# Two transformer parts on one core: the order around the unnormalised blocks, and fp32 matmuls of 256 columns issued as two of 128

## The chip, the cores and the metric

The kernel runs on one core of one Trainium2 chip. The metric is the device time of one execution in microseconds (us). All work is fp32 in the reference; the kernel holds everything in one program for one core.

## The reference

The input is one sequence of 256 tokens of width 1024. A first part of two layers is followed by two hybrid layers.

```python
for layer in range(2):
    shift_m, scale_m, gate_m, shift_f, scale_f, gate_f = ada_mod(c, ada_w[layer], ada_b[layer])
    h = modulate(rms_norm(x, norm_gains[layer, 0]), shift_m, scale_m)
    y = attn_hybrid_mixer(...) if layer == 0 else retention_mixer(...)
    x = x + gate_m * y
    h = modulate(rms_norm(x, norm_gains[layer, 1]), shift_f, scale_f)
    x = x + gate_f * swiglu(h, ffn_w_gate_up[layer], ffn_w_down[layer])
...
return rms_norm(x, final_norm)
```

`rms_norm` divides each token by the root of the mean of its squares and multiplies with a gain; `modulate(h, shift, scale)` is `h * (1 + scale) + shift`; `swiglu` is `(silu(h @ gate) * (h @ up)) @ down`, 2816 wide. `retention_mixer` projects h to q, k, v and g, turns q and k by position, and runs retention over four heads. Each hybrid layer joins a convolution branch, a latent attention branch (eight heads, `mla`) and a dilated attention branch (24 heads, `dil`) behind one normalised input and one wide projection.

## The kernel before, in words

x is kept transposed, as 8 tiles of 128 features by 256 tokens. A weight block is 128 x 1024 numbers, that is eight 128 x 128 tiles. There are 444 blocks, which pass through four slots. SyncE loads a block into `raw`; ScalarE rounds it to the high part `whi` (`hi(n)`, L1149); VectorE takes the rest as the low part `wlo` (`lo(n)`, L1647). TensorE multiplies with three matmuls per weight tile, high by high, high by low and low by high (`run`, L512 to L514). The activations have high and low parts too (`h[:, k, 0:T]` and `h[:, k, T:2T]`, T = 256). These are the dense runs: 24 matmuls of 256 columns for a block with one output tile. The waits on `blk_done`, `w_lo`, `slot_free`, `un_hi`, `h_ready` and so on, written out by hand on each engine, and the order of the instructions in each engine's queue set the order of all work.

An output tile lies in one of two banks of PSUM (`G`, by the parity of its number g). TensorE may write a bank again once `slot_free` tells that the tile two before has been read. `S` has three banks, used by attention scores and, in bank 2, by the sum of squares of x (a matmul with a matrix of ones), from which ScalarE makes the reciprocal root of the mean (`root`, L1157 and L1159).

At two places the first four blocks of a projection start before the root is known: at the retention projection (B_RET) behind the first down projection, and at the second gate/up projection (B_FFN1) behind the retention's output projection. `run_unnormed` multiplies them with x times gain, unnormalised (258 columns: 256 tokens, and the shift as two more). Its first pass covers blocks e = 0 and 1 together over k = 0 to 7 (L615), then comes the sum of squares (L618, L620), the low matmuls of both (L625), and then blocks 2 and 3 (L633 to L635). The ends are taken out of PSUM by `raw_out` (L1318 and L1319) on ScalarE and multiplied with the root later by `by_root` (L1903) on VectorE. Meanwhile `entry_norm` on VectorE makes the normalised tiles, `sq` (L1892) and from these the low parts of `h` (L1897), while `norm_hi` on ScalarE makes the high parts (L1168); block 4 is the first that uses them. At B_FFN1 the first two gate/up pairs go through `by_root`, a silu and `up_gate` (L1981) before the loop over the others starts.

`x_update` on VectorE adds each finished tile of a down or output projection to x (L1850), makes the low part of the unnormalised tile (`un_low`, L1831) and adds its squares up (L1838); `x_squares` on ScalarE makes the high part (L1301) and the squares (L1152). Between them VectorE works off dot products for the modulation vectors (`ada_later`, L1655), at blocks given by tables such as DOWN0_DOTS.

Small fp32 matmuls, not split into parts, stand between the dense runs of 24: `ret_sum` and `ret_scores` in retention; `d_sums` (a sum of squares over a head, 256 columns, L1017), `mla_scores` (128 and 256 columns, L1048 and L1049), `mla_transposes` (four of 128 columns, L1009) and others in the hybrid layers.

Of the kernel before, what the change touches and what calls it, by code (L numbers as in the profile page):

```python
# [125 lines left out]
DOWN0_DOTS = {2 * n: [57 + n] for n in range(11)}  # L126
# [67 lines left out]
def build(nc, a, out):  # L194
# [8 lines left out]
    with ctx:  # L203
# [289 lines left out]
        def _(pe):  # L493
# [109 lines left out]
            def run_unnormed(b, g, n, src):  # L603


                o = [G[:, (g + e) % 2, 0:U_WIDE] for e in range(2)]
                for e in range(2):
                    pe.wait_ge(slot_free[(g + e - 2) % 4], taken(g + e - 2))
                pe.wait_ge(w_lo, b + 2)
                pe.wait_ge(shift_lo, n + 1)  # L610
                for k in range(KT):
                    pe.wait_ge(un_hi, 8 * n + k + 1)
# [4 lines left out]
                pe.wait_ge(sq_summed, n + 2)  # L617
                pe.matmul(S[:, 2, 0:T], ones[:, :], sq[:, 0, :], start=True, stop=False)  # L618
                pe.wait_ge(sq_ready, 8 * (n + 2) + KT)
                pe.matmul(S[:, 2, 0:T], ones[:, :], sq[:, KT - 1, :], start=False, stop=True).then_inc(ss_done, 1)  # L620
# [7 lines left out]
                for e in (2, 3):  # L628
                    pe.wait_ge(slot_free[(g + e - 2) % 4], taken(g + e - 2))
                    pe.wait_ge(w_lo, b + e + 1)  # L630
                    for k in range(KT):
                        wh, wl = (w[:, (b + e) % 4, k * P:(k + 1) * P] for w in (whi, wlo))
                        pe.matmul(o[e - 2], wh, src[:, k, 0:U_WIDE], start=(k == 0), stop=False)  # L633
                        pe.matmul(o[e - 2], wh, src[:, k, U_LOW:U_LOW + U_WIDE], start=False, stop=False)
                        ins = pe.matmul(o[e - 2], wl, src[:, k, 0:U_WIDE], start=False, stop=(k == KT - 1))  # L635
# [257 lines left out]

            def ret_sum(hh):

                slot = use_t()
                pe.wait_ge(r_added, hh + 1)
                pe.matmul(Tp[:, slot, 0:T], ones[:, :], sq[:, 4, :], start=True, stop=True).then_inc(t_done, 1)
# [26 lines left out]
            for l in range(LAYERS2):  # L925
# [28 lines left out]
                def entry_sums():  # L954
# [3 lines left out]
                    pe.matmul(S[:, 2, 0:T], ones[:, :], sq[:, 0, :], start=True, stop=False)  # L958
                    ins = pe.matmul(S[:, 2, 0:T], ones[:, :], sq[:, KT - 1, :], start=False, stop=True)
                    if l == 0:  # L960
                        pe.wait_ge(sqf_summed, 1)
                        pe.wait_ge(sqf_ready, 8)
                        pe.matmul(S[:, 1, 0:T], ones[:, :], sqf[:, 0, :], start=True, stop=False)
                        ins = pe.matmul(S[:, 1, 0:T], ones[:, :], sqf[:, KT - 1, :], start=False, stop=True)
# [1546 lines left out]
```

## Time and profile before

| | |
|---|---|
| median of 3 runs | 1472.85 us (1468.15 to 1475.81) |
| profiled execution, its own time | 1468.51 us |
| its span, first to last instruction | 1466.7 us |
| TensorE busy | 1438.4 us, 98% |
| VectorE busy | 1043.1 us, 71% |
| ScalarE busy | 849.5 us, 58% |
| GpSimd busy | 93.6 us, 6% |
| mean granted TensorE clock | 0.998 of full |

The profile is of one execution. Busy time of TensorE counts overlapping matmuls once, and a matmul's duration is longer than the distance from its start to the next one's, since matmuls are pipelined. So in what follows time on TensorE is read from start to start, or as idle time ahead of an instruction.

### The profile page before, as it was taken

Reading aid. Unit: us, or ns where it says so; the run is one execution under the profiler, and the core shown is the slowest. Engines: PE = TensorE matmul, PEld = TensorE weight load, DVE = VectorE, ACT = ScalarE, POOL = GpSimd, SP = SyncE. Lnnn points to the kernel's source line nnn. Section 1 sums busy time; section 2 is a strip of 40 time slices with the busy share of each in tenths; the row PEclk is TensorE's granted clock in tenths of the full one; section 3 lists DMA queues with packets and bytes.
Section 4 is the critical chain, followed back from the end, with each engine's and each line's share of the span. In section 5 each row is a group of like instructions: output and inputs, shape, how many; then the busy total and the mean of one; then the engine's idle time right before and its main releaser. Section 6 shows DMA issues by size and latency. Waiting matters only on the chain.

```text
span 1466.7 us, 30157 instructions
## 1 busy us (share of the span) xinstructions
PE 1438.4 (98%) x11556; PEld 1361.7 (93%) x11556; DVE 1043.1 (71%) x1861; ACT 849.5 (58%) x1482; POOL 93.6 (6%) x136
## 2 busy tenths in 40 slices
PE   8999999998999999999999999999999999999999
PEld 6887999998979998999998989899999898989999
DVE  2888898887786677755665857886676684787664
ACT  4565666555556656445565766565566576656553
POOL 0111011110000000000020000230000000031000
PEclk9999999999999999999999999999999999999999
DMA  9866699996675465666663555336666355433663
GB/s 364 324 211 220 225 331 339 343 329 202 217 229 154 134 202 182 210 195 193 195 234 113 172 160 158 93 111 196 194 193 214 106 170 170 144 102 121 193 194 126
DMA packets 81185, 292.04 MB, mean 199 GB/s; under 512 B 9185, under 2 KB 10465, under 8 KB 80946
## 3 DMA queue, kind: packets, MB, share of 16 engines
q1 hardware_dynamic: 68274, 244.31, 51.4%
q0 software_dynamic: 11792, 42.77, 8.8%
q10 hardware_dynamic: 1008, 3.41, 0.7%
q8 instruction: 79, 1.29, 0.4%
q14 instruction: 32, 0.26, 0.1%
HBM read 289.40 MB, written 1.05 MB: 198 GB/s over the span
## 4 chain that ended last, share of the span: by engine, by line
PE 85%; DVE 9%; ACT 3%; issue 2%; DMA 0%; SPq 0%; DVEq 0%; ACTq 0%
PE G L512 21%; PE G L513 21%; PE G L514 21%; DVE wlo L1647 3%; PE G L571 3%; PE G L573 3%; PE G L572 3%; PE Tp L1017 1%; ACT whi L1149 1%; PE O L1093 1%; PE G L593 1%; PE Tp L945 1%; PE S L995 1%; DVE aw L1655 1%; PE Tp L685 1%
## 5 line engine op out<-in xcount | busy, mean ns | idle before, releaser
L1647 DVE TENSOR_TENSOR wlo<-raw,whi 128x1024 fp32r<-128x1024 f32 x444 | 545.4, 1231 | 261.0 <-ACT whi L1149 259.3
L512 PE MATMUL G<-h,whi 128*128 128x256 f32 x2064 | 587.2, 284 | 8.6 <-DVE wlo L1647 2.3
L1149 ACT ACTIVATE whi<-raw 128x1024 fp32r<-128x1024 f32 x444 | 468.9, 1058 | 216.6 <-PE G L514 161.6
L513 PE MATMUL G<-h,whi 128*128 128x256 f32 x2064 | 571.7, 277 | 0.0
L514 PE MATMUL G<-h,wlo 128*128 128x256 f32 x2064 | 571.6, 277 | 0.0
L512 PEld LDWEIGHTS G<-h,whi 128*128 128x128 f32 x2064 | 388.0, 188 | 16.4 <-issue 5.0
L513 PEld LDWEIGHTS G<-h,whi 128*128 128x128 f32 x2064 | 388.1, 188 | 1.8 <-issue 0.5
L514 PEld LDWEIGHTS G<-h,wlo 128*128 128x128 f32 x2064 | 387.7, 188 | 0.0
L1655 DVE CUSTOM_DVE_ANT_0 aw<-aw,cs,cols 128x1024 f32<-128x1024 f32 x80 | 101.4, 1279 | 0.0
L512 PE MATMUL G<-ah,whi 128*128 128x256 f32 x352 | 97.2, 276 | 0.0
L513 PE MATMUL G<-ah,whi 128*128 128x256 f32 x352 | 97.2, 276 | 0.0
L514 PE MATMUL G<-ah,wlo 128*128 128x256 f32 x352 | 97.2, 276 | 0.0
L488 POOL TENSOR_TENSOR bias<-dist,slopes 128x256 f32<-128x256 f32 (+1 forms) x48 | 48.7, 1030 | 533.2 <-DVE mn L2248 524.8
L512 PE MATMUL G<-yh,whi 128*128 128x256 f32 x288 | 79.9, 277 | 0.0
L513 PE MATMUL G<-yh,whi 128*128 128x256 f32 x288 | 79.5, 276 | 0.0
L514 PE MATMUL G<-yh,wlo 128*128 128x256 f32 x288 | 79.5, 276 | 0.0
L571 PE MATMUL G<-whi,h 128*128 128x512 f32 x192 | 76.9, 401 | 0.9 <-ACT rv L1182 0.5
L471 POOL DMA_DIRECT2D aw<-in_ada x80 | 42.5, 532 | 544.8 <-DVE mod L1655 510.8
L573 PE MATMUL G<-wlo,h 128*128 128x512 f32 x192 | 75.7, 394 | 0.0
L572 PE MATMUL G<-whi,h 128*128 128x512 f32 x192 | 75.5, 393 | 0.0
L513 PEld LDWEIGHTS G<-ah,whi 128*128 128x128 f32 x352 | 66.1, 188 | 0.0
L512 PEld LDWEIGHTS G<-ah,whi 128*128 128x128 f32 x352 | 66.1, 188 | 0.0
(393 smaller groups left out, 2314.4 us busy)
## 6 DMA issues: line engine op xcount, KB each, us to landing
raw<-in_w SPq DMA_DIRECT2D x444, 512.0 KB, 4.1
aw<-in_ada POOLq DMA_DIRECT2D x80, 512.0 KB, 5.2
adaw<-in_ada SPq DMA_DIRECT2D x8, 1024.0 KB, 15.3
sn<-in_uq ACTq DMA_DIRECT2D x2, 768.0 KB, 4.6
x<-in_x SPq DMA_DIRECT2D x1, 1024.0 KB, 5.2
pt<-in_ukv ACTq DMA_DIRECT2D x2, 512.0 KB, 5.8
out<-x SPq DMA_DIRECT2D x4, 256.0 KB, 2.3
dec<-in_dec ACTq DMA_DIRECT2D x1, 512.0 KB, 7.2
```

Of the source, the lines that this page charges most:

```text
L471: pool.dma_start(aw[:, r % ADA_SLOTS, :], a["ada"][16 + r]).then_inc(ada_raw[r % ADA_SLOTS], 16)
L488: pool.tensor_tensor(bias[:, DIST[grp]], dist[:, DIST[grp]], slopes[:, c:c + 1].broadcast_to([P, w]), ALU.mult).then_inc(bias_ready, 1)
L512: pe.matmul(o, wh, mv[:, 0:T], start=(k == 0), stop=False)
L513: pe.matmul(o, wh, mv[:, T:2 * T], start=False, stop=False)
L514: ins = pe.matmul(o, wl, mv[:, 0:T], start=False, stop=(k == k_of - 1))
L571: pe.matmul(o, hh, wh, start=(k == 0), stop=False)
L572: pe.matmul(o, hl, wh, start=False, stop=False)
L573: ins = pe.matmul(o, hh, wl, start=False, stop=(k == KT - 1))
L593: pe.matmul(o[n], w[:, slot, k * P:(k + 1) * P], src[:, k, 0:T], start=(k == 0 and w is whi), stop=False)
L1149: act.activation(whi[:, s, :], raw[:, s, :], ACT.Copy).then_inc(w_hi, 1)
L1647: dve.tensor_tensor(wlo[:, s, :], raw[:, s, :], whi[:, s, :], ALU.subtract).then_inc(w_lo, 1)
L1655: return dve.tensor_tensor_reduce(out=w, in0=w, in1=cs[:, :], scale=1.0, scalar=cols[:, C_ADAB + n:C_ADAB + n + 1], op0=ALU.mult, op1=ALU.add,
```

## The change

It has these parts.

1. `run_unnormed`: block 1's output goes to bank 0 of S in place of the other bank of G, and TensorE waits ahead of the first pass for one bank only. The sum of squares moves ahead of k = 7 of the first pass.
2. ScalarE: the root moves ahead of the first `raw_out`; copies out, high parts and weight splits are dealt anew. The first looped gate/up group of B_FFN1 is written out, with the second `ah` activation put into it.
3. VectorE: `x_update` adds a tile's squares behind its `un_low`, no longer ahead of the next x tile; the eleven dots of the down projection stand at blocks 0, 1, 2, 4, ... 18 in place of 0, 2, ... 20. `entry_norm` splits block b + 5 between h tiles 3 and 4; the splits of blocks 6 and 7 and the products with the root are dealt anew.
4. `in_halves`: fp32 matmuls of 256 columns in `d_sums`, `mla_scores`, `ret_sum` and `entry_sums` are issued as two of 128.

```diff
-DOWN0_DOTS = {2 * n: [57 + n] for n in range(11)}
+DOWN0_DOTS = {b: [57 + n] for n, b in enumerate((0, 1, 2, 4, 6, 8, 10, 12, 14, 16, 18))}
...
-                o = [G[:, (g + e) % 2, 0:U_WIDE] for e in range(2)]
-                for e in range(2):
-                    pe.wait_ge(slot_free[(g + e - 2) % 4], taken(g + e - 2))
+                o = [G[:, g % 2, 0:U_WIDE], S[:, 0, 0:U_WIDE]]
+                pe.wait_ge(slot_free[(g - 2) % 4], taken(g - 2))
                 pe.wait_ge(w_lo, b + 2)
                 pe.wait_ge(shift_lo, n + 1)
                 for k in range(KT):
+                    if k == KT - 1:
+                        pe.wait_ge(sq_summed, n + 2)
+                        pe.matmul(S[:, 2, 0:T], ones[:, :], sq[:, 0, :], start=True, stop=False)
+                        pe.wait_ge(sq_ready, 8 * (n + 2) + KT)
+                        pe.matmul(S[:, 2, 0:T], ones[:, :], sq[:, KT - 1, :], start=False, stop=True).then_inc(ss_done, 1)
                     pe.wait_ge(un_hi, 8 * n + k + 1)
...
+            def in_halves(to, w, moving, start):
+
+                for o in (0, P):
+                    ins = pe.matmul(to[:, o:o + P], w, moving[:, o:o + P], start=start, stop=True)
+                return ins
...
-                    pe.matmul(Tp[:, slot, 0:T], bones[:, :], sq[:, j % 8, :], start=True, stop=True).then_inc(t_done, 1)
+                    in_halves(Tp[:, slot, 0:T], bones[:, :], sq[:, j % 8, :], True).then_inc(t_done, 1)
...
             hi(B_RET + 3)
+            root(2)
             raw_out(B_RET, G_RET, 0, rqk[:, 0, :])
+            hi(B_RET + 4)
             raw_out(B_RET, G_RET, 1, rqk[:, 1, :])
-            root(2)
-            hi(B_RET + 4)
             norm_hi(16, 16, 48, range(4))
             hi(B_RET + 5)
+            raw_out(B_RET, G_RET, 2, rqk[:, 2, :])
             norm_hi(16, 16, 48, range(4, KT))
...
-                            if m >= 2:
+                            if m >= 2 and not unnormed:
                                 add_squares(m - 1)
...
                         un_low(ends.index(bb))
+                        if 1 <= ends.index(bb) < KT - 1:
+                            add_squares(ends.index(bb))
...
                 for k in range(KT):
+                    if k == 4:
+                        lo(b + 5)
                     dve.wait_ge(hi_ready, 8 * n - 8 + k + 1)
...
-            by_root(rqk[:, 0, :], G_RET).then_inc(q_scaled, 1)
-            by_root(rqk[:, 1, :], G_RET + 1).then_inc(q_scaled, 1)
-            lo(B_RET + 5)
-            for b in (2, 3):
+            for b in range(4):
+                if b < 2:
+                    lo(B_RET + b + 6)
                 by_root(rqk[:, b, :], G_RET + b).then_inc(q_scaled, 1)
-                lo(B_RET + b + 4)
```

ScalarE's queue at B_RET, before, from the last weight rounding ahead of the copies out (`whi`, L1149), over the copies (`hb` and `rqk`), to the root (`rstd`) and the high parts of h:

```order
L1149 ACTIVATE whi<-raw 128x1024
L1318 ACTIVATE hb<-G 128x1
L1319 ACTIVATE rqk<-G 128x256
L1318 ACTIVATE hb<-G 128x1
L1319 ACTIVATE rqk<-G 128x256
L1157 ACTIVATE rstd<-S 128x256
L1159 ACTIVATE rstd<-rstd 128x256
L1149 ACTIVATE whi<-raw 128x1024
L1168 ACTIVATE h<-sq,mod 128x256 x4
L1149 ACTIVATE whi<-raw 128x1024
L1168 ACTIVATE h<-sq,mod 128x256 x4
```

The same place after the change, where the lines have other numbers (L1158 is `hi`, L1166 and L1168 the root, L1328 and L1329 `raw_out`, L1177 `norm_hi`):

```order
L1158 ACTIVATE whi<-raw 128x1024
L1166 ACTIVATE rstd<-S 128x256
L1168 ACTIVATE rstd<-rstd 128x256
L1328 ACTIVATE hb<-G 128x1
L1329 ACTIVATE rqk<-G 128x256
L1158 ACTIVATE whi<-raw 128x1024
L1328 ACTIVATE hb<-S 128x1
L1329 ACTIVATE rqk<-S 128x256
L1177 ACTIVATE h<-sq,mod 128x256 x4
L1158 ACTIVATE whi<-raw 128x1024
L1328 ACTIVATE hb<-G 128x1
L1329 ACTIVATE rqk<-G 128x256
```

The root stands ahead of all copies, the second copy reads S, and the third copy stands ahead of the last four h tiles.

VectorE's queue at B_RET, before, from the last dot (`aw`) and the last update of x to the first products with the root (`rqk`):

```order
L1655 ISA aw,mod<-aw,cs,cols 128x1024
L1655 ISA mod 128x1
L1838 TENSOR_TENSOR sq<-sq 128x256
L1850 SCALAR_TENSOR_TENSOR x<-G,mod,x 128x256
L1831 SCALAR_TENSOR_TENSOR yr<-x,modA,yr 128x256
L1647 TENSOR_TENSOR wlo<-raw,whi 128x1024
L1892 SCALAR_TENSOR_TENSOR sq<-x,modA,rstd 128x256 x8
L1647 TENSOR_TENSOR wlo<-raw,whi 128x1024
L1897 SCALAR_TENSOR_TENSOR h<-sq,mod,h 128x256 x8
L1903 TENSOR_TENSOR rqk<-rqk,rstd 128x256 x2
```

The same place after (L1670 is `lo`, L1873 the update of x, L1854 `un_low`, L1917 and L1924 `entry_norm`, L1930 `by_root`):

```order
L1670 TENSOR_TENSOR wlo<-raw,whi 128x1024
L1873 SCALAR_TENSOR_TENSOR x<-G,mod,x 128x256
L1854 SCALAR_TENSOR_TENSOR yr<-x,modA,yr 128x256
L1670 TENSOR_TENSOR wlo<-raw,whi 128x1024
L1917 SCALAR_TENSOR_TENSOR sq<-x,modA,rstd 128x256 x8
L1670 TENSOR_TENSOR wlo<-raw,whi 128x1024
L1924 SCALAR_TENSOR_TENSOR h<-sq,mod,h 128x256 x4
L1670 TENSOR_TENSOR wlo<-raw,whi 128x1024
L1924 SCALAR_TENSOR_TENSOR h<-sq,mod,h 128x256 x4
L1670 TENSOR_TENSOR wlo<-raw,whi 128x1024
L1930 TENSOR_TENSOR rqk<-rqk,rstd 128x256
```

The dot and the sum of squares no longer stand ahead of the last update of x, and a split stands in the middle of the h tiles.

## Rows read from the trace of the kernel before

**Rows 1.** The page: span, the chain that ended last, one dense group.

```profile
span 1466.7 us, 30157 instructions
...
PE 85%; DVE 9%; ACT 3%; issue 2%; DMA 0%; SPq 0%; DVEq 0%; ACTq 0%
...
L513 PE MATMUL G<-h,whi 128*128 128x256 f32 x2064 | 571.7, 277 | 0.0
```

**Rows 2.** Timeline of TensorE at B_RET: start us, us, [idle before <-releaser].

```profile
346.52 0.28 PE L514 MATMUL G<-ah,wlo 128*128 128x256 f32 x1
348.53 0.36 PE L615 MATMUL G<-yr,whi 128*128 128x258 f32 x1 [1.74 <-issue]
...
362.12 0.39 PE L512 MATMUL G<-h,whi 128*128 128x256 f32 x1 [0.88 <-ACT rqk L1319]
...
366.20 0.36 PE L512 MATMUL G<-h,whi 128*128 128x256 f32 x1 [1.08 <-DVE wlo L1647]
```

**Rows 3.** Timeline of TensorE at B_FFN1.

```profile
548.87 0.28 PE L514 MATMUL G<-yr,wlo 128*128 128x256 f32 x1
549.77 0.36 PE L615 MATMUL G<-ah,whi 128*128 128x258 f32 x1 [0.62 <-issue]
...
563.35 0.38 PE L512 MATMUL G<-h,whi 128*128 128x256 f32 x1 [0.92 <-ACT sg L1319]
...
567.42 0.36 PE L512 MATMUL G<-h,whi 128*128 128x256 f32 x1 [0.98 <-DVE wlo L1647]
...
571.91 0.38 PE L512 MATMUL G<-h,whi 128*128 128x256 f32 x1 [1.52 <-ACT sg L1326]
```

**Rows 4.** The chain that ended last, at B_RET: start us, us, what.

```profile
348.53 4.11 PE G L615 x32
...
353.51 1.95 PE G L625 x16
...
356.23 0.43 ACT rstd L1159
356.68 3.26 DVE sq L1892 x8
359.94 1.14 DVE wlo L1647
361.08 3.17 DVE h L1897 x8
```

**Rows 5.** Timeline of VectorE ahead of B_RET.

```profile
346.41 1.28 DVE L1655 CUSTOM_DVE_ANT_0 aw<-aw,cs,cols 128x1024 f32<-128x1024 f32 x1
...
347.95 0.47 DVE L1850 SCALAR_TENSOR_TENSOR x<-G,mod,x 128x256 f32<-128x256 f32 x1
```

**Rows 6.** Timeline of ScalarE, at B_RET and at B_FFN1.

```profile
357.51 1.69 ACT L1168 ACTIVATE h<-sq,mod 128x256 fp32r<-128x256 f32 x4
...
565.53 1.28 ACT L1408 ACT_TABLE_LOAD   x1
```

**Rows 7.** Windows of TensorE: busy us (matmuls), granted clock, DMA share, GB/s.

```profile
521.00:548.00 27.00, 27.00 (x232) 1.00 0.68 218
600.00:627.00 27.00, 27.00 (x241) 1.00 0.63 194
```

**Rows 8.** Timeline of TensorE around three `d_sums` of the second hybrid layer.

```profile
1188.33 0.60 PE L1017 MATMUL Tp<-sq,bones 128*128 128x256 f32 x2
...
1191.49 0.59 PE L1017 MATMUL Tp<-sq,bones 128*128 128x256 f32 x2
1191.74 0.47 PE L512 MATMUL G<-h,whi 128*128 128x256 f32 x1
...
1194.75 0.38 PE L1017 MATMUL Tp<-sq,bones 128*128 128x256 f32 x1
```

**Rows 9.** Timeline of TensorE around one `mla_transposes`, four matmuls of 128 columns.

```profile
837.71 0.60 PE L1009 MATMUL Tp<-ident,qk 128*96 128x128 f32 x4
838.07 0.37 PE L512 MATMUL G<-h,whi 128*128 128x256 f32 x1
```

More of the change, by code:

```diff
@@ L897, in ret_sum @@
                 pe.wait_ge(r_added, hh + 1)
-                pe.matmul(Tp[:, slot, 0:T], ones[:, :], sq[:, 4, :], start=True, stop=True).then_inc(t_done, 1)
+                in_halves(Tp[:, slot, 0:T], ones[:, :], sq[:, 4, :], True).then_inc(t_done, 1)
             for b in range(48):
@@ L957, in entry_sums @@
                     pe.wait_ge(sq_ready, 8 * (5 + l))
-                    pe.matmul(S[:, 2, 0:T], ones[:, :], sq[:, 0, :], start=True, stop=False)
-                    ins = pe.matmul(S[:, 2, 0:T], ones[:, :], sq[:, KT - 1, :], start=False, stop=True)
+                    for o in (0, P):
+                        pe.matmul(S[:, 2, o:o + P], ones[:, :], sq[:, 0, o:o + P], start=True, stop=False)
+                        ins = pe.matmul(S[:, 2, o:o + P], ones[:, :], sq[:, KT - 1, o:o + P], start=False, stop=True)
                     if l == 0:
@@ L962, in entry_sums @@
                         pe.wait_ge(sqf_ready, 8)
-                        pe.matmul(S[:, 1, 0:T], ones[:, :], sqf[:, 0, :], start=True, stop=False)
-                        ins = pe.matmul(S[:, 1, 0:T], ones[:, :], sqf[:, KT - 1, :], start=False, stop=True)
+                        for o in (0, P):
+                            pe.matmul(S[:, 1, o:o + P], ones[:, :], sqf[:, 0, o:o + P], start=True, stop=False)
+                            ins = pe.matmul(S[:, 1, o:o + P], ones[:, :], sqf[:, KT - 1, o:o + P], start=False, stop=True)
                     ins.then_inc(ss_done, 1)
@@ L1395, in _ @@
             hi(B_FFN1 + 3)
+            root(3)
             raw_out(B_FFN1, G_FFN1, 0, sg[:, 0, :])
+            hi(B_FFN1 + 4)
             raw_out(B_FFN1, G_FFN1, 1, af[:, 0, :])
-            root(3)
-            hi(B_FFN1 + 4)
             norm_hi(24, 24, 72, range(4))
             hi(B_FFN1 + 5)
+            raw_out(B_FFN1, G_FFN1, 2, sg[:, 1, :])
             norm_hi(24, 24, 72, range(4, KT))
-            for b in (2, 3):
-                raw_out(B_FFN1, G_FFN1, b, (sg if b == 2 else af)[:, 1, :])
-                hi(B_FFN1 + b + 4)
+            raw_out(B_FFN1, G_FFN1, 3, af[:, 1, :])
+            hi(B_FFN1 + 6)
             for q in range(2):
@@ L1408, in _, with early_high @@
                 act.activation(sg[:, q, :], sg[:, q, :], ACT.Silu, bias=scol[:, 2 * q:2 * q + 1]).then_inc(gate_silu, 1)
-            for q in range(2):
+            hi(B_FFN1 + 7)
+            def early_high(q):
                 act.wait_ge(up_done, q + 1)
                 act.activation(ah[:, q, 0:T], af[:, q, :], ACT.Copy).then_inc(ah_hi, 1)
-            ffn(B_FFN1, G_FFN1, 1)
+            early_high(0)
+            gate_up(B_FFN1, G_FFN1, 1, between=lambda: early_high(1))
+            ffn(B_FFN1, G_FFN1, 2)
             def entry_tile(l, m, g, r4):
```

51 lines of the change are left out of this document (26 added, 25 removed).

## The prediction, made before the changed kernel had run

> **What bounds the kernel now.** I read the page first. TensorE is busy in nearly the whole span and the chain of work that ended last lies on it for 85% of the time [rows 1]. So the kernel is bound by TensorE, and only two things can shorten it: less time for the same matmuls, or fewer stretches in which TensorE waits. The granted clock is 1.00, the 2.4 GHz level, in every stretch I looked at [rows 7], so the clock is no lever.
>
> Then I read TensorE's timeline around the two places where `run_unnormed` stands, since the change rewrites them. At the first (B_RET) the last matmul of the down projection starts at 346.52 and the first of the unnormalised blocks at 348.53. Later block 4 starts at 362.12 after 0.88 us idle, and block 5 at 366.20 after 1.08 us idle [rows 2]. The first break is 2.01 us from start to start with 1.74 us idle; inside a dense run that distance is at most 0.12 us, so a break costs 2.01 - 0.12 - 1.74 = 0.15 us beyond its idle time. The three then cost 3.70 + 0.45 = 4.2 us. At the second place (B_FFN1) there are four, with 0.62, 0.92, 0.98 and 1.52 us idle [rows 3]: 4.04 + 0.60 = 4.6 us. Together 8.8 us, the most that the new order can bring.
>
> What ends those waits is in the chain [rows 4]. The 32 matmuls of the first pass take 4.11 us, the sum of squares stands behind them (0.87 us, from 352.64 to 353.51), then 16 low matmuls take 1.95 us. Only then, behind two copies out, comes the root on ScalarE (ends 356.66), and from there VectorE alone carries the chain: eight scaled tiles 3.26 us, a weight split 1.14 us, eight h tiles 3.17 us. The first wait has another cause. VectorE runs a dot of 1.28 us from 346.41 and updates the last x tile only from 347.95 to 348.42 [rows 5]; TensorE starts 0.11 us after that, since its second output goes to the bank which that update reads.
>
> **The change, part by part.**
>
> *The second output moves to a bank of S.* TensorE no longer waits for the last x tile at the start. It starts at about 346.7 at the first place, which saves 1.8 us, and some 0.75 us at the second. The tile is needed at k = 7, after 28 of 32 matmuls, 28/32 x 4.11 = 3.6 us later (350.3). With the last dot taken away, VectorE can update x at 346.9 (0.47 us), and ScalarE needs two activations of 0.42 us (1.69 / 4, [rows 6]): ready at about 348.3, so nothing waits. The dots moved to the first blocks cost VectorE 1.28 us each in stretches of three blocks (8.2 us) where it has room. Without it TensorE would lose at most their length, 2.6 us.
>
> *The sum of squares moves ahead of k = 7, and the root ahead of the copies.* The sum ends at 351.2 instead of 353.5, its result is there some 0.2 us later, and VectorE begins its tiles at about 352.2 instead of 356.68. That is 4.5 us earlier, of which 1.8 is TensorE's earlier start.
>
> Now TensorE's own time against VectorE's. TensorE: k = 7 and the 16 low matmuls to 353.6, then 48 matmuls of blocks 2 and 3 at 0.121 us each (1.95 / 16) to 359.4. VectorE: 352.2 + 3.26 = 355.4, split for block 4 to 356.6, h 0 to 3 to 358.2, split for block 5 to 359.3, h 4 to 7 to 360.9. TensorE reaches h tile 4 at 359.4 + 12 x 0.113 = 360.8 and the tile was ready at about 359.8: no wait. Block 5 starts at 362.1 with its weights long there. Both later waits go.
>
> What is late next is the bank for block 6 (wanted at 364.9). It is freed by ScalarE's copy of block 4, which stands behind the four bias additions, and these wait for VectorE's four products with the root: VectorE has a split (1.14), a product (0.33), a split (1.14) and three products (1.0) behind h 7, so 364.8, then one bias and one copy (0.8): 365.6. **A new wait of about 0.75 us; the first place brings 4.2 - 0.75 = 3.4 us.**
>
> At the second place the same arithmetic starts 0.75 us earlier: last matmul at 548.87, squares at 552.6, VectorE's tiles from 554.6, blocks 2 and 3 done at 561.7, blocks 4 and 5 without a wait to 567.1. The table load of 1.28 us on ScalarE [rows 6] now ends at about 564.6, and the silu behind it holds VectorE for 0.8 us. Its chain of 15.5 us of work (3.2 + 1.1 + 3.2 + 1.1, products, gates, four more splits, lows) plus 0.8 brings the bank of the first looped up block free at 571.1. TensorE wants it at 569.9. Of 4.6 us I leave 1.2: **3.4 us.**
>
> *Two of 128 for one of 256.* The code's fp32 matmul shows as two instructions in the profile. 74 are halved: 48 in `d_sums`, 16 in `mla_scores`, 4 in `ret_sum`, 6 in `entry_sums`. The direct cost: the pair of 256 starts 0.25 us ahead of the next matmul, which then takes 0.47 us, 0.72 in all [rows 8]. Four of 128 start 0.36 us ahead of one that takes 0.37 us, 0.73 in all [rows 9]. So 0.01 us each, 0.7 us for 74.
>
> The possible return is a pace. Dense runs go at one of two: in 27 us TensorE ran 232 matmuls in one stretch and 241 in others, all at full clock [rows 7], 3.8% apart (0.118 and 0.113 us start to start). Behind `d_sums` the pace alternates: from one to the next it is 3.16 us, then 3.26 us [rows 8], so a slow block of 24 costs 0.10 us. So it goes on through both layers: 14 of the 28 stretches directly behind a `d_sums` are slow, the last of them behind 1191.49. Behind four 128-column matmuls the next matmul is short and the stretch fast [rows 9], always in both layers (8 of 8), though each had a `d_sums` ahead of them. Halving it could turn all 14 (1.4 us) and, if `mla_scores` behaves the same, some 8 stretches' worth more (0.8 us). Bounds: -2.2 + 0.7 = -1.5 us if all turn fast; +0.7 us if the alternation stays; +2.1 us if every stretch turns slow (14 more). I take -0.6, nearer to rows 9, which are the same stream but for being transposes.
>
> The Trainium skill (TensorE: Matmul & The Clock Gate, "Back-to-back issue gap") gives a gap of N/2.4 + 2.5 ns, so every extra matmul instruction costs 2.5 ns and the same columns never get cheaper by being cut: an estimate by it is 74 x 2 x 2.5 ns = 0.4 us lost and none returned, a total of -6.4 us. [...]
>
> **Sum.** -3.4 - 3.4 - 0.6 = -7.4 us. The profiled execution took 1468.5 us (span 1466.7 and 1.8 around it), so it would take 1461.1. That execution stands at the low end of the runs shown, 4.3 us under their median of 1472.85; moved along, the median becomes **1465 us**.
>
> **Rivals.** *The supply takes the place of the waits* (chance 0.19). ScalarE and VectorE get no lighter, and at both places they run nearly without pause for 12 us. If raw copies and splits queue a little worse than I count, only the starts are gained, 1.8 + 0.75, with 1 us of the rest: -3.5 us, 1469.
>
> *A long stretch changes pace* (0.19). From 571.91, after a wait of 1.52 us [rows 3], to the end of the down projection some 163 us later, TensorE ran at the fast pace (600 to 627 in rows 7 is of it). With that wait changed it may settle at the slow one: 163 x 3.8% = +6.2 us, so -1.2 us in all, 1471.5. For it: half of the stretches behind `d_sums` are slow, and the stretch from 521 to 548 [rows 7] stayed slow for long. Against: after most waits the fast one set in.
>
> *Everything comes* (0.13): no new waits, all stretches fast: -8.8 - 1.5 = -10.3 us, 1462.5.
>
> *Slower* (0.05): the slow pace takes the long stretches of the last layers too. There are 3 x 2064 = 6192 matmuls on h [rows 1]; if 4000 of them, those behind the first changed place by my estimate, ran at 0.118 in place of 0.113 us (3.8%, 0.0043 us each), that is +17.2 us, so 1482.5. The time is above before's once 7.4 / 0.0043 = 1700 have turned, and by over 0.5% from 3400.
>
> *Forecast* (0.44): 1465, its own range 1461.5 to 1468.5.
>
> **Range and chances.** The tails take the slow-stretch case in and leave out the slower one: 1459 to 1472. 0.5% is 7.4 us, about what a measurement of this kernel can tell from no change, and the forecast lies on it. Faster by more: 0.7 of the forecast and the whole of the everything case, 0.44. Slower by more: 0.05. Within: 0.51.
>
> **What would show it.** In the changed profile: the first unnormalised matmul within 0.3 us of the last one of the down projection; the root ending by 352.2; no break ahead of blocks 4 and 5; a short one ahead of block 6 and one of about 1 us in the first looped gate/up group; `d_sums` as four instructions, and the distance between them 3.17 us at every one that only a block of 24 parts. Wrong would make it: matmuls of 0.28 us that run at 0.118 start to start after 571, breaks at k = 7, or `d_sums` distances that alternate still.

## The result, and the profile after

The changed kernel took 1464.58 us in the median of 12 runs (1461.10 to 1468.31), before 1474.92 us beside it; the ratio is 0.9935, 95% interval 0.9917 to 0.9953. Timed twice more, unchanged, it gave 0.9963 (0.9942 to 0.9985) and 1.0006 (0.9984 to 1.0027). The mean of the three ratios is 0.9968, 4.7 us. The ratios stand as they were recorded with their intervals and are not quotients of the two medians. So the first result stands at the favourable end of what the change is worth, and a good part of this text is about why three such measurements differ.

The page of the profiled execution, which took 1464.42 us, to be read against [rows 1]:

```profile
span 1462.6 us, 30445 instructions
...
PE 89%; DVE 7%; ACT 2%; issue 2%; DMA 0%; SPq 0%; DVEq 0%; ACTq 0%
...
L513 PE MATMUL G<-h,whi 128*128 128x256 f32 x2064 | 572.8, 278 | 0.0
```

TensorE now carries 89% of the chain, VectorE 7% instead of 9%. But the same 2064 matmuls last 278 ns in the mean instead of 277: something was given back inside the dense runs.

TensorE's timeline at B_RET and B_FFN1 after the change (columns as in [rows 2]):

```profile
346.68 0.28 PE L514 MATMUL G<-ah,wlo 128*128 128x256 f32 x1
346.79 0.28 PE L619 MATMUL G<-yr,whi 128*128 128x258 f32 x1
...
365.58 0.38 PE L512 MATMUL G<-h,whi 128*128 128x256 f32 x1 [0.69 <-ACT rqk L1401]
...
544.05 0.28 PE L619 MATMUL G<-ah,whi 128*128 128x258 f32 x1
...
565.97 0.39 PE L512 MATMUL G<-h,whi 128*128 128x256 f32 x1 [1.06 <-DVE af L1901]
```

Of seven breaks two are left. The first unnormalised matmul starts 0.11 us behind the last one of the down projection, where it was 2.01 us [rows 2]. Blocks 4 and 5 have none, at either place; block 6 has one at B_RET, block 7 one at B_FFN1.

The chain at B_RET, then ScalarE's and VectorE's timelines there, to be read against [rows 4] and [rows 5]:

```profile
350.33 0.43 PE S L613 x2
350.76 0.43 PE S L615 x2
```

```profile
351.23 0.38 ACT L1166 ACTIVATE rstd<-S 128x256 f32<-128x256 f32 x1 [1.96 <-PE S L615]
351.65 0.42 ACT L1168 ACTIVATE rstd<-rstd 128x256 f32<-128x256 f32 x1
...
363.95 1.31 ACT L1372 ACTIVATE rqk<-rqk,hb 128x256 f32<-128x256 f32 x3 [0.96 <-DVE rqk L1930]
365.17 0.36 ACT L1401 ACTIVATE rqk<-G 128x256 f32<-128x256 f32 x1
```

```profile
346.99 0.48 DVE L1873 SCALAR_TENSOR_TENSOR x<-G,mod,x 128x256 f32<-128x256 f32 x1 [0.34 <-PE G L514]
...
352.10 3.26 DVE L1917 SCALAR_TENSOR_TENSOR sq<-x,modA,rstd 128x256 f32<-128x256 f32 x8 [1.56 <-ACT rstd L1168]
...
363.50 1.09 DVE L1930 TENSOR_TENSOR rqk<-rqk,rstd 128x256 f32<-128x256 f32 x3
```

The last x tile is updated from 346.99 to 347.47 us while TensorE is already in the first pass. The sum of squares ends at 351.19, VectorE starts its eight tiles at 352.10 where it was 356.68. The last lines of both engines are the new wait: products to 364.59, bias additions to 365.26, the copy that frees the bank to 365.53, and TensorE 0.05 us after it.

### The profile page after: what moved, and what is told of

Same layout as the page of the kernel before. It is cut to its first block, busy times and chain, and to the rows that moved or that the text cites. A ratio compares the mean times of both kernels' runs of the same rounds, so it can differ in the third digit from the quotient of the medians.

```text
span 1462.6 us, 30445 instructions
## 1 busy us (share of the span) xinstructions
PE 1441.0 (99%) x11704; PEld 1371.9 (94%) x11704; DVE 1043.7 (71%) x1861; ACT 848.6 (58%) x1482; POOL 92.0 (6%) x136
## 4 chain that ended last, share of the span: by engine, by line
PE 89%; DVE 7%; ACT 2%; issue 2%; DMA 0%; SPq 0%; DVEq 0%; ACTq 0%
PE G L512 22%; PE G L513 22%; PE G L514 22%; PE G L571 3%; PE G L572 3%; PE G L573 3%; DVE wlo L1670 2%; PE Tp L898 2%; PE O L1102 1%; PE G L593 1%; ACT whi L1158 1%; PE Tp L952 1%; PE S L1004 1%; DVE aw L1678 1%; PE Tp L686 1%
## 5 line engine op out<-in xcount | busy, mean ns | idle before, releaser
L1670 DVE TENSOR_TENSOR wlo<-raw,whi 128x1024 fp32r<-128x1024 f32 x444 | 546.0, 1232 | 257.2 <-ACT whi L1158 255.4
L1158 ACT ACTIVATE whi<-raw 128x1024 fp32r<-128x1024 f32 x444 | 468.8, 1058 | 216.7 <-PE G L514 160.7
L512 PE MATMUL G<-h,whi 128*128 128x256 f32 x2064 | 583.5, 283 | 4.8 <-DVE at L2319 1.6
L514 PE MATMUL G<-h,wlo 128*128 128x256 f32 x2064 | 572.8, 278 | 0.0
L512 PEld LDWEIGHTS G<-h,whi 128*128 128x128 f32 x2064 | 389.4, 189 | 10.6 <-issue 2.2
L514 PEld LDWEIGHTS G<-h,wlo 128*128 128x128 f32 x2064 | 387.8, 188 | 0.0
L512 PE MATMUL G<-ah,whi 128*128 128x256 f32 x352 | 97.2, 276 | 0.0
L514 PE MATMUL G<-ah,wlo 128*128 128x256 f32 x352 | 97.2, 276 | 0.0
L512 PE MATMUL G<-yh,whi 128*128 128x256 f32 x288 | 80.2, 278 | 0.0
L514 PE MATMUL G<-yh,wlo 128*128 128x256 f32 x288 | 80.0, 278 | 0.0
L571 PE MATMUL G<-whi,h 128*128 128x512 f32 x192 | 76.8, 400 | 1.4 <-ACT mqk L1267 1.4
L573 PE MATMUL G<-wlo,h 128*128 128x512 f32 x192 | 75.6, 394 | 0.0
L512 PEld LDWEIGHTS G<-ah,whi 128*128 128x128 f32 x352 | 66.1, 188 | 0.0
```

The lines of the kernel that those rows point to most:

```text
L512: pe.matmul(o, wh, mv[:, 0:T], start=(k == 0), stop=False)
L514: ins = pe.matmul(o, wl, mv[:, 0:T], start=False, stop=(k == k_of - 1))
L571: pe.matmul(o, hh, wh, start=(k == 0), stop=False)
L573: ins = pe.matmul(o, hh, wl, start=False, stop=(k == KT - 1))
L1158: act.activation(whi[:, s, :], raw[:, s, :], ACT.Copy).then_inc(w_hi, 1)
L1670: dve.tensor_tensor(wlo[:, s, :], raw[:, s, :], whi[:, s, :], ALU.subtract).then_inc(w_lo, 1)
```

## The experiments

**How they are compared.** The spread of the runs of one program (7 to 18 us in these measurements) is larger than most effects here. The traces show what makes up most of it from one profiled execution to another; the other executions have no trace. In a dense run the next matmul starts either 112 to 115 ns or 116 to 119 ns after the one before, and a long run stays with one distance for hundreds of matmuls. In this text these two distances are the two paces, and a start of the second kind is a slow start. Windows of 27 us in after, one in the loop behind B_FFN1 and one in the merge of the first hybrid layer (about 975 to 1080 us), then the second window in the kernel before:

```profile
600.00:627.00 27.00, 27.00 (x241) 1.00 0.60 193
990.00:1017.00 27.00, 27.00 (x232) 1.00 0.59 188
```

```profile
990.00:1017.00 27.00, 27.00 (x241) 1.00 0.65 198
```

The clock is granted in full (1.00) in all of them. So beside the times I give for each profile the span less 4.4 ns (118 less 113.6) for each slow start, counted over the whole trace, called here the span at one pace. (A count over all matmuls, whatever their shape, is 106 to 132 starts higher, in all profiles nearly alike.) It still holds waits that differ from one execution to another of kernels that are alike there: up to 1.1 us ahead of 340 us and up to 1.6 us between the two changed places, among them one of the retention (ahead of L571, at about 418 us). So it is good to some 1 to 2 us only. The last three columns leave these waits out: the matmuls of the dense runs (L512 to L514) are matched one to one with those of the kernel before, slow starts counted out, and each column is what a profile gained on before in one stretch, from 340 to 380 us (B_RET), from 548 to 580 us (B_FFN1) and from 580 us to the end, by before's times.

| profile | span | slow starts | span at one pace | B_RET | B_FFN1 | behind 580 |
|---|---|---|---|---|---|---|
| before | 1466.7 | 1548 | 1459.9 | | | |
| f4_before_again | 1467.0 | 1802 | 1459.1 | 0.0 | 0.1 | 0.0 |
| f1_order_only | 1460.2 | 1836 | 1452.1 | 3.5 | 3.7 | 0.0 |
| f2_halves_only | 1475.4 | 3365 | 1460.6 | 0.1 | 0.1 | -0.9 |
| after | 1462.6 | 2317 | 1452.4 | 3.5 | 3.8 | -1.0 |
| f3_after_again | 1466.1 | 2974 | 1453.0 | 3.5 | 3.8 | -1.1 |
| h5_after_third | 1463.2 | 2002 | 1454.4 | 3.5 | 3.7 | -0.9 |
| g1_bank_only | 1465.9 | 2121 | 1456.6 | 2.0 | 1.0 | 0.1 |
| g2_sum_and_root_first | 1470.4 | 3267 | 1456.0 | 2.2 | 2.4 | 0.1 |
| g3_order_plus | 1458.9 | 1752 | 1451.2 | 4.4 | 4.6 | -0.4 |
| h2_order_tuned | 1459.5 | 1649 | 1452.2 | 4.5 | 4.4 | -0.5 |
| h3_tuned_steered | 1470.2 | 3935 | 1452.9 | 4.0 | 4.0 | -1.4 |
| h4_before_steered | 1485.9 | 5528 | 1461.6 | -0.3 | -0.5 | -1.0 |

My theory: the order is worth what its breaks were, and the halves cost a little and return nothing. Rivals: the gain comes from the pace, by the halves or by chance; the bank alone or the earlier root alone makes it.

### The order alone, the halves alone, and both kernels again

f1_order_only is after with `in_halves` taken out:

```diff
-                    in_halves(Tp[:, slot, 0:T], bones[:, :], sq[:, j % 8, :], True).then_inc(t_done, 1)
+                    pe.matmul(Tp[:, slot, 0:T], bones[:, :], sq[:, j % 8, :], start=True, stop=True).then_inc(t_done, 1)
```

and so in `mla_scores`, `ret_sum` and `entry_sums`. f2_halves_only is the kernel before with the same lines the other way round. f3_after_again and f4_before_again are after and before unchanged.

> The new order (parts 1 to 3) with the fp32 matmuls left whole at 256 columns. Theory: nearly all of the gain is the removed breaks. The changed kernel's profile had matmuls of the same ordinal 3.3 us earlier behind the first place and 3.7 us earlier over the second one. So this kernel's profile shows about 7 us won at the two places, breaks of about 0.9 us at block 6 (first place) and 1.2 us at block 7 (second place) left, and a time 6 to 9 us under before. Rival (the halved matmuls carry a good part of the 9.5 us): only 3 to 5 us under before.

> The kernel before, with only the fp32 matmuls of 256 columns halved (d_sums, mla_scores, ret_sum, entry_sums). Theory: nothing, within 1.5 us of before, since the stretches behind a lone d_sums turn fast (14 slow ones, 1.4 us) while the eight behind d_sums and four transposes turn slow (0.8 us) and the halving costs 0.01 us each (0.7 us). Rival (the halves set the pace of the long stretches too): 3 us or more under before, with no slow stretch of over 100 matmuls in the hybrid layers.

> The changed kernel once more, unaltered. Theory (the pace of a long stretch is drawn anew in each execution): the stretch of 888 matmuls in the first hybrid layer's merge, slow in the first profile (3.7 us), is fast in this one or other long stretches are slow, and the ratio to before is 0.993 to 0.996. Rival (the pace is fixed by the program): the same stretches slow as in the first profile, to the matmul.

> The kernel before once more, unaltered. Theory (pace drawn anew): long stretches change pace against the first profile, whose span of 1466.7 us was at the low end of its runs (1468 to 1483 us); a typical execution has one or two more long stretches slow and a span of about 1472. Rival (fixed by the program): the same slow stretches, and the longer runs come from elsewhere, such as longer breaks.

Measured beside 1470.07 us of before: order alone 1463.16 us (12 runs), ratio 0.9967 (0.9941 to 0.9993); halves alone 1471.28 us, ratio 1.0016 (0.9993 to 1.0039); after 1470.34 us, ratio 1.0006; before again 1468.82 us, one run. The order brings 3.5 and 3.7 us at the two places, **7.2 us**, and nothing behind them. The halves cost 0.9 to 1.1 us behind 580 us, where 70 of the 74 lie, in each of the four profiles that have them, with slow starts counted out. The timed runs don't resolve so little: the interval of the halves alone takes in a ratio of 1.

The profiles of f3 and f4 went as neither of their theories said. The slow stretch of after's first profile was slow again in f3, but two others, at 140 to 163 and 502 to 550 us, were slow in it besides; f4's span was 1467.0 us and not 1472, with 254 slow starts more than the first profile of before. So the pace of a stretch is not fixed by the program alone. The clearest case is the longest stretch, the feed-forward loop of layer 0 (about 173 to 347 us, some 1540 starts, 6.8 us between the paces), ahead of which no kernel but the last two (h3 and h4) differs from before: it was fast in ten of these twelve profiles and slow in f2 and g2, which makes their long spans. A window of it in f2, where before has 241 matmuls at the same place:

```profile
200.00:227.00 27.00, 27.00 (x232) 1.00 0.93 328
```

What the halves do is in TensorE's timeline of after around `d_sums` (L898; `mla_transposes` is L1018), to be read against [rows 8] and [rows 9]:

```profile
1186.37 0.60 PE L898 MATMUL Tp<-sq,bones 128*128 128x128 f32 x4
...
1189.55 0.60 PE L898 MATMUL Tp<-sq,bones 128*128 128x128 f32 x4
...
1192.73 0.60 PE L898 MATMUL Tp<-sq,bones 128*128 128x128 f32 x4
1193.17 0.60 PE L1018 MATMUL Tp<-ident,qk 128*96 128x128 f32 x4
...
1196.44 0.61 PE L898 MATMUL Tp<-sq,bones 128*128 128x128 f32 x4
1196.88 0.60 PE L1018 MATMUL Tp<-ident,qk 128*96 128x128 f32 x4
...
1200.15 0.61 PE L898 MATMUL Tp<-sq,bones 128*128 128x128 f32 x4
```

and the same place in the kernel before:

```profile
1201.53 0.59 PE L1017 MATMUL Tp<-sq,bones 128*128 128x256 f32 x2
1201.96 0.60 PE L1009 MATMUL Tp<-ident,qk 128*96 128x128 f32 x4
...
1205.13 0.59 PE L1017 MATMUL Tp<-sq,bones 128*128 128x256 f32 x2
```

The distance between lone `d_sums` is 3.18 to 3.19 us at all 28 of both layers: no more 3.17 and 3.26 in turn. That was forecast. But where transposes follow, the distance went from 3.60 to 3.71 us: behind `mla_transposes` 8 stretches of 8 are slow now. Four more turned slow behind the second and third `d_sums` of each layer, beside which the sums of the latent branch (`lora_sums`) stand: 3.61 to 3.71 and 3.93 to 4.04 us. The first kind won 0.9 us in all, the second lost 0.9, the third 0.4. Added up over both layers, the distances between `d_sums`, their pace and the cost of the halves included, grew by 0.4 to 0.5 us; those between `mla_scores` stayed the same to 0.2 us.

### The order's two parts

g1_bank_only is the kernel before with the second output in S, and its copy out taken from there; g2_sum_and_root_first is the kernel before with the sum ahead of k = 7 and the root ahead of the first copy (so too at B_FFN1, with `root(3)`):

```diff
-                o = [G[:, (g + e) % 2, 0:U_WIDE] for e in range(2)]
-                for e in range(2):
-                    pe.wait_ge(slot_free[(g + e - 2) % 4], taken(g + e - 2))
+                o = [G[:, g % 2, 0:U_WIDE], S[:, 0, 0:U_WIDE]]
+                pe.wait_ge(slot_free[(g - 2) % 4], taken(g - 2))
```

```diff
+                    if k == KT - 1:
+                        pe.wait_ge(sq_summed, n + 2)
+                        pe.matmul(S[:, 2, 0:T], ones[:, :], sq[:, 0, :], start=True, stop=False)
...
+            root(2)
             raw_out(B_RET, G_RET, 0, rqk[:, 0, :])
             raw_out(B_RET, G_RET, 1, rqk[:, 1, :])
-            root(2)
```

> The kernel before with one part of the new order: the second unnormalised output in a bank of S, so that TensorE waits for one bank only. Theory (the first break is the wait for the bank of the last x tile, and everything behind moves with it): the first breaks at both places go (1.74 and 0.62 us idle), the others stay as they were (0.9 and 1.1; 0.9, 1.0 and 1.5 us idle), so 2.6 us won in the profile. Rival (the dot on VectorE, 1.28 us ahead of the last x tile, is what costs): TensorE then breaks at k = 7 and less than 1.5 us is won.

> The kernel before with the other part alone: the sum of squares ahead of k = 7 and the root ahead of the copies out, all banks and all other orders as before. Theory: VectorE's tiles start 2.8 us earlier against TensorE's first pass, so at the first place both later breaks go (2.3 us won) and at the second some 2.8 of 3.8 us; the first breaks stay (1.74 and 0.62 us idle). About 5 us won in the profile. Rival (VectorE's own work is the bound whatever the root does): the breaks ahead of blocks 4 and 5 shrink by less than half.

Measured beside 1475.12 us of before: 1468.56 us, ratio 0.9968 (0.9947 to 0.9989), and 1471.23 us, ratio 0.9974 (0.9952 to 0.9996). TensorE in g1, at B_RET and B_FFN1:

```profile
361.44 0.39 PE L512 MATMUL G<-h,whi 128*128 128x256 f32 x1 [0.88 <-ACT rqk L1320]
365.52 0.36 PE L512 MATMUL G<-h,whi 128*128 128x256 f32 x1 [1.07 <-DVE wlo L1648]
```

```profile
561.25 0.38 PE L512 MATMUL G<-h,whi 128*128 128x256 f32 x1 [0.88 <-ACT sg L1320]
565.32 0.36 PE L512 MATMUL G<-h,whi 128*128 128x256 f32 x1 [0.99 <-DVE wlo L1648]
```

The first breaks are gone, and the later waits are as long as before (0.88, 1.08 us in [rows 2], 0.92, 0.98 in [rows 3]). By matched matmuls the bank brings 2.0 us at B_RET and 1.0 at B_FFN1, 3.0 where its theory had 2.6. (The waits at B_RET come only 0.7 us earlier than in before, since this execution lay 1.3 us behind it at 340 us, by a slow stretch ahead.) In g2 TensorE still waits 1.63 us at the start of B_RET:

```profile
356.92 0.36 PE L620 MATMUL G<-yr,whi 128*128 128x258 f32 x1 [1.63 <-issue]
```

The break ahead of block 5 is gone at both places and that ahead of block 4 is down to 0.14 us idle, but the last one of B_FFN1 shrank only from 1.52 to 1.16 us idle. The earlier root brings 2.2 and 2.4 us, 4.6 where its theory had about 5. Both parts are needed. Their sum is 7.6 us, a little over the 7.2 of the whole, so what the splits and the bias work, which were dealt anew as well, bring by themselves is not shown.

### The waits that are left

g3_order_plus is f1 with the bias additions moved behind block 5's copy and the silu table loaded right behind the root:

```diff
-            for b in range(4):
-                act.wait_ge(q_scaled, b + 1)
-                act.activation(rqk[:, b, :], rqk[:, b, :], ACT.Identity, bias=scol[:, b:b + 1]).then_inc(q_shifted, 1)
...
+                if b == 5:
+                    for q in range(4):
+                        act.wait_ge(q_scaled, q + 1)
...
+            act.preload_act_table_set("silu_and_others")
```

h2_order_tuned loads the table ahead of the fourth copy instead, and halves the 14 lone `d_sums` of each layer (j = 3 and 5 to 17), so that nothing with transposes behind it is halved:

```diff
-                    pe.matmul(Tp[:, slot, 0:T], bones[:, :], sq[:, j % 8, :], start=True, stop=True).then_inc(t_done, 1)
+                    if 2 < j < 18 and j not in (4,):
+                        in_halves(Tp[:, slot, 0:T], bones[:, :], sq[:, j % 8, :], True).then_inc(t_done, 1)
+                    else:
+                        pe.matmul(Tp[:, slot, 0:T], bones[:, :], sq[:, j % 8, :], start=True, stop=True)\
+                          .then_inc(t_done, 1)
```

> The new order without the halves, and the two breaks that it left taken on: the four bias additions of the retention queries stand behind block 5's copy on ScalarE, and the silu table is loaded behind the root, where ScalarE is idle for 0.6 us. Theory: the break ahead of block 6 (0.69 us idle) goes, VectorE's 0.98 us of idle time ahead of its first gate goes, and of TensorE's 1.06 us idle at the second place at most 0.3 is left: 1.6 us under the order alone in the profile, once slow stretches are counted out, and 0.990 to 0.996 of before in time. Rival (the table load now delays the copies out and the weights): a new break of up to 0.7 us in blocks 2 to 4 of the second place.

> The new order without any halved matmul except the 14 lone d_sums of each hybrid layer (those not next to a group of transposes), with the four bias additions of B_RET behind block 5's copy on ScalarE and the load of the silu table at B_FFN1 ahead of the fourth copy out instead of right behind the root. Nothing is left out. Theory (breaks are the time, the pace of long stretches is drawn anew in each execution): the break of 0.54 us that g3_order_plus had at block 2 of B_FFN1 goes, no new break over 0.3 us comes, so the span less 4.4 ns for each slow start is 1450.3 to 1450.8 us (g3: 1451.1, after: 1452.4 and 1452.9); all lone d_sums are followed by fast runs. Median 1459 to 1467, ratio to before 0.992 to 0.996. Rival (ScalarE and VectorE have no room left at B_FFN1): the break moves to blocks 6 or 7 with 0.5 to 1.3 us, span less slow starts 1451.3 or more.

Measured: g3 1466.12 us beside 1475.12, ratio 0.9941 (0.9918 to 0.9964); one execution of it and one of before took over 3700 us and are not in the ratio. h2 1465.96 us beside 1473.17, ratio 0.9942 (0.9921 to 0.9963). In g3 both breaks of after are gone, and one is new, at the third unnormalised block of B_FFN1, since the load now holds up the copy that frees its bank:

```profile
551.79 0.39 PE L634 MATMUL G<-ah,whi 128*128 128x258 f32 x1 [0.26 <-ACT sg L1327]
```

In h2 that one is gone and a smaller form of the old one is back, by TensorE's timeline:

```profile
567.16 0.39 PE L512 MATMUL G<-h,whi 128*128 128x256 f32 x1 [0.43 <-DVE af L1906]
```

By matched matmuls the two places bring 9.0 us in g3 and 8.9 in h2, where the order alone brings 7.2: 1.8 and 1.7 us more, where g3's theory had 1.6. g3 gives back 0.4 us behind 580 us, most of it in a wait at 751 us that no other profile has, and h2 0.5 us for its 28 halved matmuls. h2's theory of no break over 0.3 us was wrong: its rival, that the break moves to block 7, came with 0.6 us from start to start beyond the pace. Both have shorter spans than after, but the timed ratios of g3, h2, f1 and after overlap.

### What sets the pace

g4_double_d_sums issues every `d_sums` matmul twice (the same result written a second time):

```diff
+                    pe.matmul(Tp[:, slot, 0:T], bones[:, :], sq[:, j % 8, :], start=True, stop=True)
                     pe.matmul(Tp[:, slot, 0:T], bones[:, :], sq[:, j % 8, :], start=True, stop=True).then_inc(t_done, 1)
```

> The kernel before with each d_sums matmul of 256 columns issued twice into the same output. Theory (each fp32 matmul of 256 columns flips the pace of the dense run behind it): two leave it as it was, so the alternation behind lone d_sums goes, all have one pace. Rival (the pace depends on the distance in time or is drawn anew): slow and fast still alternate. Direct cost 48 x 0.43 = 21 us in either case, so only the pace is read from it.

Measured: 1497.29 us, one run. TensorE's timeline:

```profile
1212.48 0.60 PE L1017 MATMUL Tp<-sq,bones 128*128 128x256 f32 x2
1212.92 0.59 PE L1018 MATMUL Tp<-sq,bones 128*128 128x256 f32 x2
...
1216.18 0.60 PE L1017 MATMUL Tp<-sq,bones 128*128 128x256 f32 x2
...
1219.87 0.60 PE L1017 MATMUL Tp<-sq,bones 128*128 128x256 f32 x2
```

The distance is 3.70, then 3.69: no alternation, all slow. One fp32 matmul of 256 columns turns the pace from one stretch to the next, at 28 of 28 places in each kernel that has them whole. But two do not leave it as it was, as the theory had it: at two of the 28 places, one in each layer (the first at 780 us), the run ahead was fast (113 to 114 ns) and the one behind slow (117 to 119), and the other 26 came in slow and stayed so. Behind two the pace was slow from either. So behind such work the pace is a rule of the sequence, and it was the same in both profiles of before.

That led to a last theory, that a pair of fp32 matmuls of 128 columns leaves TensorE fast for any stretch behind it. h3_tuned_steered is h2, and h4_before_steered the kernel before, with this at five places (the products are dummies that nobody reads):

```diff
+                keep_busy(2, S[:, 0, :])
```

h5_after_third is after unchanged, measured beside them.

> As h2_order_tuned, with two more fp32 matmuls of 128 columns (dummies whose result nobody reads, 0.44 us a place) at five places: ahead of each feed-forward loop of the first part, behind the last unnormalised block's successor at B_RET, and behind the second block of the last merge of both hybrid layers. Theory A (an fp32 matmul of 128 columns leaves TensorE in the fast pace, as behind 28 of 28 lone halved d_sums, and a long stretch keeps the pace it enters with): the long stretches behind the five places are fast in every execution, fewer than 1200 slow starts in the profile against 1500 to 3300 before, runs within 3 us of each other, median 1457 to 1461 although 2.2 us of work is added. Rival B (a long stretch's pace is set by something else and drawn inside it): slow starts as before, 1500 to 3000, the same spread, and the median 2 us above h2_order_tuned.

> The kernel before with the same five pairs of dummy matmuls alone. Theory A: the long stretches are fast, fewer than 1200 slow starts, median 2 to 4 us under before, spread under 3 us. Rival B: same draw of paces as before, so 2 us slower by the added work, ratio 1.000 to 1.003.

> The changed kernel a third time, unchanged, since two calls gave 0.9935 and 1.0006. Theory (7 us of breaks are gone for good, 0.5 to 1 us is paid for the halves, and the pace of the long stretches is drawn in each execution, 1000 slow starts being 4.4 us): span less slow starts again 1452.4 to 1452.9, median 1462 to 1471, ratio 0.993 to 1.000, the mean of the three near 0.997. Rival (the first call was what the change is worth, the second disturbed): ratio 0.992 to 0.995 again with few slow starts.

Measured beside 1473.17 us of before: h3 1470.89 us, 4.9 us above h2, ratio 0.9978 (0.9953 to 1.0004), 3935 slow starts; h4 1487.60 us, ratio 1.0083 (1.0058 to 1.0108), its six runs between 1481.84 and 1489.02 us, 5528 slow starts. Theory A is wrong. Windows of h4 in the feed-forward loop of layer 1 and in the two merge stretches:

```profile
620.00:647.00 27.00, 27.00 (x232) 1.00 0.59 192
1010.00:1037.00 27.00, 27.00 (x241) 1.00 0.61 194
1390.00:1417.00 27.00, 27.00 (x232) 1.00 0.61 182
```

The loop behind B_FFN1 was fast in all other thirteen profiles. Rival B is wrong too: it had the same draw as before and 2 us. What the dummies do can be read at the places themselves. At all ten, five in each kernel, the run behind them has the other pace than the run ahead: six were fast ahead and slow behind, four slow ahead and fast behind. In the last merge stretch of h4 the dummies start at 1363.30 us; L512 ahead of them and behind them, where a duration of 276 ns goes with the fast pace and one of 281 ns with the slow one:

```profile
L512 PE MATMUL G<-h,whi x8: 276/276/385, 1360.5 to 1363.0; 128*128 128x256 f32 x8
```

```profile
L512 PE MATMUL G<-h,whi x16: 281/281/281, 1366.6 to 1371.9; 128*128 128x256 f32 x16
```

So a pair of dummies turns the pace, and does not make it fast, as a halved `d_sums` did (28 of 28 in after, 4 of them from slow), though both are four instructions of 128 columns. Most long stretches are entered fast, so they came out slow: the first feed-forward loop and the last merge stretch in both kernels, the loop behind B_FFN1 in h4. The 3726 and 3980 slow starts that h4 has more than the two profiles of before are 16 to 18 us of the 19 us by which its span is longer; the dummies' own time is some 0.5 us a pair (B_FFN1 in the table). Why dummies and halves differ stays open.

The third timing of after, 1468.12 us, fell where the theory of the drawn pace had it; its span less slow starts, 1454.4, is above the 1452.4 to 1452.9 expected. It gained as much at both places as the other two profiles of after, and the difference lies in waits elsewhere, 1.0 us of it in that of the retention:

```profile
418.24 0.50 PE L571 MATMUL G<-whi,h 128*128 128x512 f32 x1 [0.87 <-ACT rv L1191]
```

### Where the merge stretch turned

In the three profiles of after the first merge stretch (885 starts) is slow, and so it is in g4; h3 and h4 entered it slow as well and were turned fast by their dummies. In the eight others it is fast. That is 885 x 4.4 ns = 3.9 us, as much as half of the order's gain. The place where f1 and after part can be read, since behind a wait of TensorE for the dilated attention (`sn`) come the same eight transposes, a block of 24 and the same 24 small matmuls. f1_order_only, then after:

```profile
969.65 1.09 PE L952 MATMUL Tp<-ident,sn 128*128 128x128 f32 x8 [0.46 <-DVE sn L2284]
970.50 0.36 PE L512 MATMUL G<-h,whi 128*128 128x256 f32 x1
...
973.50 1.96 PE L1100 MATMUL O<-pt,dv 128*64 128x256 f32 x24
```

```profile
968.22 1.09 PE L952 MATMUL Tp<-ident,sn 128*128 128x128 f32 x8 [0.45 <-DVE sn L2286]
969.07 0.36 PE L512 MATMUL G<-h,whi 128*128 128x256 f32 x1
...
971.99 1.96 PE L1102 MATMUL O<-pt,dv 128*64 128x256 f32 x24
```

Behind the wait the block takes 3.00 us in f1 (slow) and 2.92 us in after (fast). The 24 small matmuls turn the pace, so that the long stretch behind them is fast in f1 and slow in after. The same was so in all fourteen profiles: eight with a slow block came out fast, six with a fast block slow. TensorE stood idle for 0.46 and 0.45 us; the length of the wait does not tell the two apart: from start to start it was 725 to 758 ns in the eight, 730 to 741 in the six.

## Why the prediction was right, and where it was not

**The breaks at the start, and blocks 4 and 5: right.** The first matmul came at 346.79 against 346.7, VectorE's tiles began at 352.10 against 352.2, TensorE's later waits of 0.88 and 1.08 us went. No break came at k = 7: the x tile was done at 347.47, TensorE wanted it behind 350.33.

**What is late next: right in kind.** At B_RET the wait of 0.75 us ahead of block 6, behind the bias additions, came as 0.97 us from start to start, 0.85 us more than inside a run, from the engines and instructions named. Matched matmul by matmul, after gained 3.5 us on before at this place, against 3.4. At B_FFN1 I left 1.2 us; it was one break of 1.33 us, 1.2 beyond the pace. VectorE waits 0.98 us behind the table load where I had 0.8:

```profile
558.13 1.28 ACT L1425 ACT_TABLE_LOAD   x1
```

```profile
549.36 3.26 DVE L1917 SCALAR_TENSOR_TENSOR sq<-x,modA,rstd 128x256 f32<-128x256 f32 x8 [1.56 <-ACT rstd L1168]
...
560.04 0.49 DVE L2006 SCALAR_TENSOR_TENSOR af<-af,hb,sg 128x256 f32<-128x256 f32 x1 [0.98 <-ACT sg L1425]
```

The second place brought 3.8 us by matched matmuls, against 3.4. The two terms, -6.8 us, measured 7.2 by themselves in f1.

**The halves: wrong, in sign.** I took -0.6 us, a direct cost of 0.7 less a return of 1.3 by the pace of short stretches. The direct cost was somewhat larger, 0.9 to 1.1 us with the pace counted out. The return was not there: with the pace counted in, the distances between `d_sums` and between `mla_scores` grew by some 0.4 us together. So the step "nearer to rows 9, which are the same stream but for being transposes" failed. The stretches in [rows 9] were fast because a whole fp32 matmul of 256 columns stood ahead of the four transposes; with that halved, the same transposes are followed by a slow stretch. The 0.9 us that the lone `d_sums` won were lost there and beside `lora_sums`.

**A long stretch changes pace: I had it as a rival, at another place.** I looked for it behind 571.91, where it did not come in after. It came in the merge stretch of the first hybrid layer, 3.9 us in place of 6.2. In the profiled executions after was 8.6 us ahead of before at matched matmuls at 840 us, 4.7 behind the merge, 4.1 at the end. Its time was 1464.42, 4.1 us under before's, not the 7.4 of the sum. The median agreed with 1465 in part by luck: before's profiled execution was a lucky one, as the prediction said, and the first measurement was favourable to after. There the medians lay 10.3 us apart; timed again, after's median was 1470.34 us, 0.3 above before's, and 1468.12 us, 5.1 under it. What is right beyond luck are the breaks, read one by one. The 4.1 us of the profiled executions add up: 7.2 at the two places and 1.3 in waits between them that came out shorter, less 1.0 for the halves, and 3.4 less for 769 slow starts more. Whether the halves cause the slow merge is not shown: three of three profiles with both order and halves have it, none of the order or the halves alone, and g4 and h4, which have none of the halves, entered it slow too, as did h3 with 28 of them. Timed runs of after go down to 1461.10, about f1's lowest (1461.01), so it can hardly be in every execution.

**Supply, and slower: did not happen.** ScalarE and VectorE worked as counted.

## What to carry to other kernels

Where one engine carries the chain, count its breaks from start to start, follow each to the late engine, and then ask what is late next: here that gave 7.2 us to within 0.4. Do not book a gain on a pattern in the stream (what follows what) unless the trace holds the very sequence that the change makes, with what stands ahead of it; the stretch behind `d_sums` and transposes had only been seen with a whole matmul ahead. And where the spread of a program's runs is as large as the effect, compare the traces with the cause of the spread counted out, place by place, since waits elsewhere move the whole span by 1 to 2 us, and measure the change more than once. Here whole spans would have put the earlier root at some 3.5 us; its two places show 4.6.

## What the runs showed of the hardware that was not expected

Dense matmuls of 256 columns ran at two paces at the full granted clock, 113.6 and 118 ns from start to start; a matmul's duration in the trace shows which. L512 in the window 990 to 1017 us, of after and of f1_order_only:

```profile
L512 PE MATMUL G<-h,whi x53: 281/281/281, 989.9 to 1016.7; 128*128 128x256 f32 x53
```

```profile
L512 PE MATMUL G<-h,whi x57: 276/276/276, 989.8 to 1017.0; 128*128 128x256 f32 x57
```

The Trainium skill (TensorE: Matmul & The Clock Gate, "Back-to-back issue gap") gives 262 cycles for 256 columns, 109 ns at 2.4 GHz, as the gap of an isolated matmul; the prediction's estimate of 0.4 us goes by the formula behind it. For a stream of weight loads and matmuls the same section has other figures, 81 ns for 128 columns and 131 ns for 512. No dense run here had any of these: 256 columns took 113.6 or 118 ns, and the 512 columns of L571 to L573 took 225 to 232 ns. The measured ones decide. The pace holds through a run of any length seen (some 1540 starts). It is turned by one fp32 matmul of 256 columns and by a pair of dummies of 128, is slow behind two of 256 with no transposes behind them, and can come out either way behind a wait. Between 1548 and 5528 starts of a profile were slow, 4.4 ns each, which is 17.5 us between the two ends. What in the chip makes these two paces, and what decides behind a wait, stays open.
